# Layer 0: the sampled tokens' attention over cached pages is run in phases inside the prompt attention's steps

## The reference, cut to what matters

```python
k_past = gather_pages(past['cache_fox_k'][e], page_table)   # 16 pages of 128 tokens a sequence
v_past = gather_pages(past['cache_fox_v'][e], page_table)
...
k_all = jnp.concatenate([k_past, k], axis=1)
v_all = jnp.concatenate([v_past, v], axis=1)
o_fox = fox_attention(q, k_all, v_all, lf_all, pos0).reshape(B, T, FOX_WIDTH)
...
y = jnp.concatenate([o_fox, o_pool], axis=-1) @ w_out
```

## Time and profile before

| | us |
|---|---|
| median of three runs | 2513.2 |
| lowest, highest run | 2511.01, 2521.77 |
| the profiled execution, its own time | 2518.82 |
| span of its trace | 2517.1 |
| prompt attention, from its block's first record to its last | 255.1 to 321.1 |
| decode, from its first record to its last | 324.0 to 515.5 |

### The profile page before, as it was taken

How to read it: one execution, slowest core, us unless ns; L and a number is a source line. 1 busy time by engine, 2 the same in 40 slices (tenths; PEclk the granted TensorE clock), 3 DMA queues, 4 the chain that set the end, 5 groups by cost and what they waited for, 6 DMA issues and landing times. The chain is left out here.

```text
span 2517.1 us, 48020 instructions
## 1 busy us (share of the span) xinstructions
PE 2130.6 (85%) x17829; PEld 1906.4 (76%) x17829; DVE 1206.8 (48%) x2282; ACT 578.9 (23%) x1074; POOL 265.0 (11%) x429
## 2 busy tenths in 40 slices
PE   4887746787999899698779995998977687999898
PEld 2873622375999899698459895988974387999898
DVE  4334711155444443433545657877743356444433
ACT  2210500012101000201136664444431212101000
POOL 0100234300000000000012222212223100000000
PEclk8986877887999999799779997998988898999999
DMA  9315189934332231223440003433448612323221
GB/s 355 108 50 233 36 309 386 376 122 134 87 88 85 84 104 54 62 69 119 193 152 2 1 1 102 121 115 103 121 158 317 222 63 79 92 83 91 87 93 59
DMA packets 237432, 322.05 MB, mean 128 GB/s; under 512 B 18235, under 2 KB 194440, under 8 KB 229807
## 3 DMA queue, kind: packets, MB, share of 16 engines
q1 hardware_dynamic: 215191, 239.29, 28.6%
q0 software_dynamic: 22048, 80.24, 9.1%
HBM read 311.56 MB, written 16.42 MB: 130 GB/s over the span
## 5 line engine op out<-in xcount | busy, mean ns | idle before, releaser
L441 PE MATMUL ps<-XHup,WHup 128*128 128x272 f32 x1408 | 293.6, 290 | 16.9 <-DVE XLup L415 13.4
L441 PE MATMUL ps<-XHup,WLup 128*128 128x272 f32 x1408 | 292.9, 290 | 0.0
L441 PE MATMUL ps<-XLup,WHup 128*128 128x272 f32 x1408 | 292.1, 289 | 0.0
L2168 PE MATMUL ps<-CHi,W1H 128*128 128x256 f32 x768 | 221.8, 289 | 38.2 <-DVE CLo L2271 38.1
L441 PEld LDWEIGHTS ps<-XHup,WHup 128*128 128x128 f32 x1408 | 223.2, 190 | 19.8 <-DVE XLup L415 14.2
L441 PEld LDWEIGHTS ps<-XLup,WHup 128*128 128x128 f32 x1408 | 223.1, 190 | 0.0
L441 PEld LDWEIGHTS ps<-XHup,WLup 128*128 128x128 f32 x1408 | 221.5, 190 | 0.0
L2169 PE MATMUL ps<-CLo,W1H 128*128 128x256 f32 x768 | 219.8, 286 | 0.0
L2170 PE MATMUL ps<-CHi,W1L 128*128 128x256 f32 x768 | 219.6, 286 | 0.0
L2168 PEld LDWEIGHTS ps<-CHi,W1H 128*128 128x128 f32 x768 | 150.0, 195 | 40.2 <-DVE CLo L2271 29.8
L434 DVE CAST WHup<-RAWup 128x1024 fp32r<-128x1024 f32 x88 | 61.1, 695 | 221.6 <-DMA RAWup<-in_w_up 163.4
(11 more groups left out here) (499 smaller groups left out, 4184.9 us busy)
## 6 DMA issues: line engine op xcount, KB each, us to landing
RAWup<-in_w_up SPq DMA_DIRECT2D x88, 512.0 KB, 3.8
Wearly<-in_w_mod SPq DMA_DIRECT2D x24, 1024.0 KB, 10.8
RAWdn<-in_w_down SPq DMA_DIRECT2D x14, 1408.0 KB, 6.1
KP<-in_cache_fox_k POOLq DMA_DIRECT2D x64, 256.0 KB, 6.1
KP<-in_cache_fox_k SPq DMA_DIRECT2D x64, 256.0 KB, 12.4
VP<-in_cache_fox_v POOLq DMA_DIRECT2D x64, 256.0 KB, 5.9
VP<-in_cache_fox_v SPq DMA_DIRECT2D x64, 256.0 KB, 12.4
RAWin<-in_nsa_w_in SPq DMA_DIRECT2D x20, 512.0 KB, 3.6
```

The source lines that it names most:

```text
L441: mm = self.nc.tensor.matmul(self.ps[:, banks + n, 0:HALF], w, x[:, n * HALF:(n + 1) * HALF], start=start, stop=stop)
L2168: nc.tensor.matmul(out, WH[:, sig, k, w], hi, start=(k == 0 and m == 0), stop=False, skip_group_check=True)
```

## The change

`fox_decode` and the block that copies `QN` and `VN` go. A class `PastAttention` holds the same computation as four generators (`pe`, `act`, `dve`, `pool`) cut into phases, and `prompt_attention` takes it as `beside`. At the end of each of its steps, every engine runs the next phase of its generator; phases left over run after the loop. Per sequence there are ten phases: four for the K page groups of sequence b+1, four for the V page groups of b, one that turns b+1's probabilities, one that spreads its maxima and turns b's heads. In all 82 phases (6 for the first K, 7 times 10, 6 for the last V) beside 58 steps.

A group is four pages, one from each quarter of a sequence: 64 groups of 1 MB. They go through a ring of four slots, two new and two in `PT`'s chunks 8 to 15. K scores are now made group by group, so a matmul has 128 moving columns where it had 512, and there are four times as many. The prompt attention gets four PSUM banks beside the phases (two for scores, one for turns, one for outputs; its combine step goes from 6 to 4), the pages get the other four. Layer 1 calls `prompt_attention` without `beside` and keeps eight.

```diff
+class PastAttention:
+    R, PAGES, QUARTERS, SLOTS = FH * TS, PAST // PAGE, 4, 4
+    S, TURN, OUT, STATS = 4, 5, 6, 7
...
+    def load(self, engine, parity, k):
+        kind, b, n = self.groups[k]
+        if k >= self.SLOTS:
+            engine.wait_ge(self.used, k - self.SLOTS + 1)
...
+        for a in range(parity, self.QUARTERS, 2):
+            at = b * self.PAGES + self.PER * a + n
+            page = engine.value_load(self.k.pages[0:1, at:at + 1], min_val=0, max_val=self.k.n_pages - 1)
+            engine.dma_start(self.slot(k)[:, a, :], pages[ds(page, 1), :, :].rearrange("a p f -> p (a f)")).then_inc(
+                (self.pool_full if parity else self.sp_full)[k % self.SLOTS], 16)
+
+    def sp(self, sp, store):
...
+        for k in range(self.SLOTS):
+            self.load(sp, 0, k)
+        store(sp)
+        for k in range(self.SLOTS, len(self.groups)):
+            self.load(sp, 0, k)
+        self.k.start_out(sp, self.k.i["ab_w_out"][0], self.first)
+
+    def pool(self, pool):
+        for k in range(self.SLOTS):
+            self.load(pool, 1, k)
+        for k in range(len(self.groups)):
+            if k + self.SLOTS < len(self.groups):
+                self.load(pool, 1, k + self.SLOTS)
+            yield
...
+        def past_scores(b, n):
+            k = self.index["k", b, n]
+            keys = self.slot(k)
+            landed(k)
+            for hp in range(4):
+                for a in range(QUARTERS):
+                    last = nc.tensor.matmul(ps[a * R:(a + 1) * R, S, n * P:(n + 1) * P], self.QBA[:, b, hp * R:(hp + 1) * R], keys[:, a, hp * P:(hp + 1) * P],
+                                            start=(hp == 0), stop=(hp == 3), skip_group_check=True)
...
+        for b in range(-1, NB):
+            if b + 1 < NB:
+                for n in range(PER):
+                    past_scores(b + 1, n)
+                    if n == PER - 1:
+                        new_scores(b + 1)
+                    yield
+            if b >= 0:
+                for n in range(PER):
+                    values(b, n)
+                    yield
+            if b + 1 < NB:
+                turn(b + 1)
+            yield
+            if b + 1 < NB:
+                spread_row(b + 1)
+                turn_new(b + 1)
+            if b >= 0:
+                turn_heads(b)
+            yield
...
-        S_BANKS, T_BANK, O_BANK = 4, 4, 6
-        TURN, COPY, PV, COMBINE, LAG = 2, 3, 4, 6, 9
+        S_BANKS, T_BANKS, O_BANKS, COMBINE = (2, 1, 1, 4) if beside else (4, 2, 2, 6)
+        T_BANK, O_BANK = S_BANKS, S_BANKS + T_BANKS
+        TURN, COPY, PV, LAG = 2, 3, 4, 9
...
+                    if beside:
+                        next(phases, None)
+                for _ in phases if beside else ():
+                    pass
...
-            self.fox_decode(QN, VN, NC, EP, first)
```

More of the change, by code:

```diff
@@ L1303, in prompt_tiles, with prompt_attention @@
         return T, {n: sem("pa_" + n) for n in names}
-    def prompt_attention(self, T, sems, groups, heads, keysets, outs, setup_dve, store):
+    def prompt_attention(self, T, sems, groups, heads, keysets, outs, setup_dve, store, beside=None):
         nc, ps = self.nc, self.ps
         QS, P3, PTB, NM, RC, O, T2, ID, MASK, KT, PC = (T[n] for n in ("QS", "P3", "PTB", "NM", "RC", "O", "T", "ID", "MASK", "KT", "PC"))
-        S_BANKS, T_BANK, O_BANK = 4, 4, 6
-        TURN, COPY, PV, COMBINE, LAG = 2, 3, 4, 6, 9
+        S_BANKS, T_BANKS, O_BANKS, COMBINE = (2, 1, 1, 4) if beside else (4, 2, 2, 6)
+        T_BANK, O_BANK = S_BANKS, S_BANKS + T_BANKS
+        TURN, COPY, PV, LAG = 2, 3, 4, 9
         units = [(g, i) for g in range(len(groups)) for i in range(PT_TILES)]
@@ L1361, in _ @@
             def _(pe):
+                if beside:
+                    phases = beside.pe(pe)
                 pe.wait_ge(sems["consts"], 1)
@@ L1398, in _ @@
                         pe.wait_ge(sems["bank_read"], made[place[n]] + 1)
-                        if n >= 2:
-                            pe.wait_ge(sems["out_dve" if by_dve[n - 2] else "out_act"], copies[n - 2])
-                        turned = ps[:, T_BANK + n % 2, :]
+                        if n >= T_BANKS:
+                            pe.wait_ge(sems["out_dve" if by_dve[n - T_BANKS] else "out_act"], copies[n - T_BANKS])
+                        turned = ps[:, T_BANK + n % T_BANKS, :]
                         if dense(g):
@@ L1412, in _ @@
                         pe.wait_ge(sems["out_dve" if by_dve[n] else "out_act"], copies[n])
-                        if i == 0 and g >= 2:
-                            pe.wait_ge(sems["combined"], g - 1)
-                        out = ps[:, O_BANK + g % 2, i * (HD + 1):(i + 1) * (HD + 1)]
+                        if i == 0 and g >= O_BANKS:
+                            pe.wait_ge(sems["combined"], g - O_BANKS + 1)
+                        out = ps[:, O_BANK + g % O_BANKS, i * (HD + 1):(i + 1) * (HD + 1)]
                         tiles = i + 1 if dense(g) else 1
@@ L1420, in _ @@
                         last.then_inc(sems["valued"], 1)
+                    if beside:
+                        next(phases, None)
+                for _ in phases if beside else ():
+                    pass
             @block.scalar
             def _(act):
+                if beside:
+                    phases = beside.act(act)
                 act.wait_ge(sems["consts"], 1)
@@ L1439, in _ @@
                         if dense(g):
-                            nc.scalar.copy(PTB[:, n % 3, 0:i + 1, :], ps[:, T_BANK + n % 2, 0:(i + 1) * P]
+                            nc.scalar.copy(PTB[:, n % 3, 0:i + 1, :], ps[:, T_BANK + n % T_BANKS, 0:(i + 1) * P]
                                            .rearrange("p (j q) -> p j q", q=P)).then_inc(sems["out_act"], 1)
@@ L1443, in _ @@
                             w = width(g, i)
-                            nc.scalar.copy(PC[0:w, n % 3, :], ps[0:w, T_BANK + n % 2, 0:P]).then_inc(sems["out_act"], 1)
+                            nc.scalar.copy(PC[0:w, n % 3, :], ps[0:w, T_BANK + n % T_BANKS, 0:P]).then_inc(sems["out_act"], 1)
                     kind, n = items[step] if step < len(items) else (None, None)
@@ L1459, in _ @@
                 link = Chain(dve, sems["dc"])
+                if beside:
+                    phases = beside.dve(dve)
                 setup_dve(dve, link)
@@ L1477, in _ @@
                             dve.wait_ge(sems["valued"], n - 2)
-                        nc.vector.tensor_copy(PTB[:, n % 3, 0:i + 1, :], ps[:, T_BANK + n % 2, 0:(i + 1) * P]
+                        nc.vector.tensor_copy(PTB[:, n % 3, 0:i + 1, :], ps[:, T_BANK + n % T_BANKS, 0:(i + 1) * P]
                                               .rearrange("p (j q) -> p j q", q=P)).then_inc(sems["out_dve"], 1)
@@ L1488, in _ @@
                         G = groups[g]
-                        rows = ps[:, O_BANK + g % 2, 0:PT_TILES * (HD + 1)].rearrange("p (i x) -> p i x", x=HD + 1)
+                        rows = ps[:, O_BANK + g % O_BANKS, 0:PT_TILES * (HD + 1)].rearrange("p (i x) -> p i x", x=HD + 1)
                         dve.wait_ge(sems["valued"], n + 1)
@@ L1508, in _ @@
                 placed = summed = 0
+                if beside:
+                    phases = beside.pool(pool)
                 for step in range(steps):
@@ L1533, in _, with fox_prompt @@
                         nc.gpsimd.tensor_tensor(dst, dst, T2[:, adds[g] % 2, :, :], ALU.add).then_inc(sems["added"], 1)
-    def fox_prompt(self, PT, TOK, NC, store):
+                    if beside:
+                        next(phases, None)
+                for _ in phases if beside else ():
+                    pass
+    def fox_prompt(self, PT, TOK, NC, EP, first, store):
         nc, H = self.nc, self.H
@@ L1538, in fox_prompt @@
             T, sems = self.prompt_tiles(sb, sem, FH * PT_TILES, [TP] * 3)
+            past = PastAttention(self, sb, sem, PT, TOK, NC, EP, first)
             VE = sb("VE", [P, PT_TILES, FH, HD + 1])
@@ L1563, in fox_prompt @@
                                    value=lambda j, h=h: VE[:, j, h, :]))
-            self.prompt_attention(T, sems, groups, heads, keysets, [H[:, c, 0:TP] for c in range(4)], setup, store)
+            self.prompt_attention(T, sems, groups, heads, keysets, [H[:, c, 0:TP] for c in range(4)], setup, lambda sp: past.sp(sp, store), past)
     def gather(self, pool, table, col, where, dst, loaded):
@@ L1800, in fox_mixer @@
             NC, EP = sb("NC", [FH, NT]), sb("EP", [P, NB, PAGE])
-            QN, VN = sb("QN", [P, 8, NS]), sb("VN", [NS, 512])
             with self.stage() as (sb2, sem2):
@@ L1810, in fox_mixer @@
                 self.pooling(PT, (self.early, 13))
-                self.fox_prompt(PT, TOK, NC, lambda sp: self.store_tokens(sp, TOK, [("fox_k", 0, 512, 0), ("fox_v", 512, 512, 0)], stored))
-                with nc.Block() as block:
-                    @block.vector
-                    def _(dve):
```

(4 more changed lines are left out.)

397 lines of the change are left out of this document (206 added, 191 removed).

## The result

The changed kernel takes 2520.96 us in the median of 13 runs (lowest 2515.79), the kernel before 2515.32 us in the same comparison: ratio 1.003, 95% interval 1.0018 to 1.0042. Run again: 2519.63 against 2516.66, ratio 1.0023 (1.0006 to 1.0041). Where 34 us were forecast to be saved, 3 to 6 are lost: both intervals lie above 1, and the loss is less than the half per cent that the prediction took as its bound.

A forecast was written before the change was run, and what follows sets the result against it. Compute-bound prompt attention and DMA-bound pages ran in turn; overlapped, TensorE bounds until 382 us (275 + 46 + 41 + 15, plus 5), then DMA, ending at 481.5 against 515.5: 34 us saved, 2479 us; 2455 to 2505 holds 8 in 10.

The forecast's parts named there:

- The stages' limits: In the kernel before, the prompt attention is bound by TensorE, the decode by DMA, one after the other.
- the K form's price: Small K score matmuls, 128 moving columns on 32 weight columns: 27 ns a record, 1.1 us a K phase.
- TensorE's phase 0: First phase of the pages' work on TensorE, which needs QBA first: put at 275 us.
- the waits of the joint stretch: TensorE waiting for ScalarE and VectorE, mostly at three heavy phases per sequence: 15 us, ends 0 and 30.
- joint stretch: Prompt attention with pages' phases beside it, first matmul to phase 33's end: 112.5 us, ending at 382.
- the sign: What would show the forecast right: waits of 1 to 3 us after each last K group, released by ScalarE's copy.
- Rival 1: DMA bounds it from the first phase, waits being hidden: 67 us saved, 2446 us; chance 0.13.
- rival 4: Small K weight loads do not overlap, 106 ns a record: 20 us slower, 2533 us; chance 0.03.
- rival 5: No overlap, as the ring gets its pages late: only the barriers' 4 us less the start, 2510; chance 0.02.
- Rival 2: Joint work of 87 us runs at the decode's clock of 0.80: 17 us saved, 2496 us; chance 0.11.
- Rival 3: Every step's turn waits through maximum, exponential and copy, 2.2 us in 33 steps: 24 us slower, 2537; chance 0.05.
- page stretch: From phase 33 to the last record, bound by page loads at 386 GB/s, four slots sufficing: 98.5 us.

The follow-up runs named there:

- little-DMA run: The changed kernel with only 16 of 128 partition rows of each page loaded from the fifth group on: 2499.34 us, one run.
- three sizes: The changed kernel with a ring of three, four and six groups: page stretch 149.2, 126.7 and 112.5 us.
- the later phases: The changed kernel with ScalarE's and VectorE's phases one step later, behind their copy of the turned probabilities: 2494.93 us against 2517.86, ratio 0.991.
- Both: The changed kernel with a ring of six groups and ScalarE's and VectorE's phases one step later: 2480.18 us against 2517.86, ratio 0.985.

## Why the prediction was wrong

**What held.** The stages' limits and the prompt's 1.46 us a step; the K form's price (31 ns measured, 27 forecast); TensorE's phase 0 (4.2 us of wait; 273.0, with step 0 1.7 us earlier than in before); the waits of the joint stretch: 15 us forecast, 15.2 measured, in ten waits of which the long ones come where copies stand behind the phase of the last K group or the turn phase. That the sums agree so closely is in part luck: 9.8 of the 15.2 us end with VectorE's copy, where I had put the longer waits and the sign on ScalarE's. The joint stretch's 7.5 us more are TensorE's busy time, 100.3 us where I had 88 (46, 41 and step 0) and 5 for the clock, which was 0.89. DMA was no limit there, as the little-DMA run shows. Rival 1 fails by that, rival 4 by the 31 ns, rival 5 by the 38 us. Rival 2 named the clock for the joint stretch, where it was 0.89 and not 0.80; the low clock, 0.69 in the mean, lay in the page stretch. Rival 3 has its mechanism, the single bank with the copy behind a phase, but in few steps and at a quarter of its price.

**The step that failed** is the page stretch: "TensorE needs 4.8 + 5.1 + 2.5 = 12.4 us per sequence, under 21.7 for eight groups, and no phase pair stops it for the 10.9 us that the ring holds; four slots suffice as 16 MB did." Three things in it:
- *The ring, 14 us.* The ring covers 10.9 us only where it is empty at the start of the gap. Part of the four groups has landed while TensorE works on the one before: 6.8 us were left at the boundary shown. And the gap was not 2.5 us but some 9 there, from the last V group's use to the first K group's, and 14.4 behind phase 33, where the prompt attention's trailing pieces lie in it too; I had put these at nothing. That the ring's size costs time is shown by its three sizes.
- *The clock.* The 12.4 us were read in a stretch of before that ran at a mean clock of 0.97 (450 to 460 us) and 0.84 (460 to 470). TensorE's busy time per sequence is 18 to 20 us at means of 0.62 to 0.74. At the boundary shown, the clock was 1.00 while TensorE was busy for 1.65 of 4.5 us, waiting for pages, then 0.55 and 0.50. At the half clock the gap is longer: a K group's 40 records take 2.3 us there (from 398.8) and 1.2 at the full clock. In a longer gap the ring runs full, so the next pages come later; that this closes a circle is argued from these rows, no run holds the clock fixed. I put 5 us for the clock on the joint stretch alone and nothing here. The little-DMA run gives a bound for all that is not bytes: 106.0 us with hardly a byte moved, against 98.5 forecast with all of them. It has clock, order and the pace of the issues in it, and these were not separated. Nor is the clock a term beside the other two: part of the ring's 14 us and of the order's 8 is busy time at a lower clock.
- *The order, 8 us.* The copy behind the phase delays the last units' turns after phase 33 too. I ended those waits at phase 33. Shown: 126.7 to 118.4, and 112.5 to 105.0; 3 us of it are the waits, 5 a higher clock in the same window.

14 and 8 make 22 of the 28 us; six slots and the later phases leave 105.0, 6.5 over the forecast, of which I have shown no single cause. That version saves about what was forecast of the change, 37.7 us between the medians of its own comparison, but not by the sum of the forecast: its joint stretch is 4.9 us under it and its page stretch 6.5 over.

## What to carry to other kernels

To size a ring, take the longest stretch in which its reader frees nothing, at the reader's slow clock, and count only what is still to land when that stretch begins: here four slots held 10.9 us, had 6.8 left, and stood against gaps of 9 and 14.4. When phases of another job are hung into a hand-written order, put each engine's phase behind the piece that another engine waits for, not at the end of the step: here that was worth 21 us in the two stretches, with nothing left out. And what one stage's overlap gains is only kept if buffers that were large (16 MB) are not paid for it (4 MB).

## What the runs showed of the hardware

- Two records of the small K form start 31 ns apart while each one's weight load of 32 columns lasts 106 ns or more: loads and matmuls of the four column strips overlap although all use the full 128 rows.
- GpSimd's issues of 256 KB pages follow each other every 1.15 us, and those of 32 KB in the little-DMA run as well, where the groups still came 1.7 to 2.6 us apart.
- The same records of TensorE took 26.2 us at a granted clock of 0.64 and 16.5 at 1.00 (the first window behind phase 33, in the change and in Both).
- The pages of the ring's two new slots landed 4.8 us after issue in the median, shortest 2.5, against 6.6 and 3.5. What shortened it was not tested:

```profile
DMA to landing us min/median/max: 2.5/4.8/8.2
```
